# High weights against high and low input in three matmuls of 288, 512 and 288 columns, low sums apart in PSUM

## The chip, the cores and the metric

One NeuronCore of a Trainium2 chip runs the whole program. The metric is the device time of one execution in microseconds. Five engines take part: TensorE (PE: matmuls, PEld: its weight loads), VectorE (DVE), ScalarE (ACT), GpSimd (POOL) and SyncE (SP, which issues the DMAs).

## The reference

One inference step of a 2-layer streaming encoder over 544 tokens (512 of a prompt, 32 of a sample), width 1024:

```python
x = x + jnp.concatenate([o_a, o_b, o_c, o_d], axis=-1) @ w_out
x = x + jnp.square(jax.nn.relu(rmsnorm(x, norm_mlp) @ mlp_w1)) @ mlp_w2
x = x + (pl @ ple_w_proj) * jax.nn.sigmoid(rmsnorm(x, norm_ple) @ ple_w_gate)
```

`o_a` to `o_d` are four head groups (gated DeltaNet, sliding-window attention, latent attention, a short gated convolution). `mlp_w1` is 1024 x 4096, `mlp_w2` 4096 x 1024, `ple_w_gate` 1024 x 1024. The inputs are float32, and so is the result.

## The kernel before

Activations lie feature-major: `x[128, 8, 544]`, features on partitions in 8 k-tiles (`KT`), tokens along the free axis. For float32 accuracy at the matmul's fast type (fp32r), each operand is split into a high part (rounded to fp32r) and a low part (what is left). A product is high x high + high x low + low x high, with the weights `whi` (high) and `wlo` (low) and the activations in `ha` and `hb`, shape `[128, 8, 2, 544]`, where index 0 of the third axis is the high part and 1 the low.

Weights come in units of 128 output features x 1024 inputs (512 KB in float32). For each unit SyncE loads `raw`, ScalarE writes `whi` (`high`, L642), GpSimd writes `wlo` (`rest`, L559), and TensorE runs `product` (L1330): for each of 8 k-tiles six matmuls of 272 columns (half of the 544 tokens, `HALF`), that is `whi` with both halves of the high part, `whi` with both halves of the low part, `wlo` with both halves of the high part, 48 in all. Both halves of a product sum up in two PSUM banks; consecutive products alternate between two pairs of banks. `raw`, `whi` and `wlo` have two slots each: the unit after next can be split only when the present product is through (ScalarE waits for `proj`), and its `wlo` must be there before its product.

A layer has 23 units of the input projection with the attention and DeltaNet work between them, then 8 of the output projection, then the MLP in 4 groups (`GROUPS`): 8 up products (`ha` to hidden features), then 8 down products (`hb` to x), and then the gates: twice four short products of the per-layer input (`ple_out`, 12 matmuls each) and four gate products of 48. Then comes the next layer, or the final norm.

The order on every engine is written out by hand and in-order; semaphores tie the engines together. What the change touches:

- TensorE: `product` L1330 (used by MLP and gates too), `sum_x` L1315 (sum of squares over the partitions for the rms), `first_units` L1350 (the next layer's first two products).
- VectorE, up products (`mlp_group`): L1180 takes relu of the PSUM sum times rms and frees the bank, L1182 squares, `split_to` casts to the high part (L914) and subtracts for the low part (L915), which signals `hidden`. The first down product waits, k-tile by k-tile, for the `hidden` tile of the same number.
- VectorE, down products: `add_out` L1167 adds the sum to x. In the last group `norm_high` (ScalarE, L659) and `norm_split` (VectorE, L909) then split x for the gates, and `square_x` (L665) and `add_square` (GpSimd, L571) sum the squares.
- VectorE, gates: L1296 multiplies the PSUM sum by rms, a memset (L1297) signals `gate_in`, ScalarE takes the sigmoid (L874), VectorE multiplies by `ple_out` (L1280) and adds to x (L1281). L1288 copies `ple_out` out of PSUM.
- GpSimd, gates: its queue alternates `rest` of a coming weight with `add_square` of a finished x tile, in that order by hand.

## Time and profile before

| | |
|---|---|
| median of 3 runs | 1681.04 us (1680.88 to 1682.52) |
| the profiled execution, its own time | 1682.13 us |
| its span (first to last instruction) | 1680.3 us |
| matmul instructions | 14582 |
| TensorE busy, share of the span | 94% |
| VectorE, ScalarE, GpSimd busy | 55%, 29%, 38% |

The page is one profiled execution. Its 40 slices are 42 us each: layer 0 takes the first 20, layer 1 the others. Matmuls overlap in the records (a matmul of 272 columns is shown with about 0.29 us, while the next one starts long before its end), so pace is read from start to start: of a merged row "start, us, xcount" it is (us minus one matmul's duration) / (count - 1). A square bracket behind a row is the idle time of that engine before it, and what ended it.

### The profile page before, as it was taken

Reading aid. Unit: us, or ns where it says so; the run is one execution under the profiler, and the core shown is the slowest. Engines: PE = TensorE matmul, PEld = TensorE weight load, DVE = VectorE, ACT = ScalarE, POOL = GpSimd, SP = SyncE. Lnnn points to the kernel's source line nnn. Section 1 sums busy time; section 2 is a strip of 40 time slices with the busy share of each in tenths; the row PEclk is TensorE's granted clock in tenths of the full one; section 3 lists DMA queues with packets and bytes.
Section 4 is the critical chain, followed back from the end, with each engine's and each line's share of the span. In section 5 each row is a group of like instructions: output and inputs, shape, how many; then the busy total and the mean of one; then the engine's idle time right before and its main releaser. Section 6 shows DMA issues by size and latency. Waiting matters only on the chain. (4 is left out here: it accounts for less than half of the span.)

```text
span 1680.3 us, 33063 instructions
## 1 busy us (share of the span) xinstructions
PE 1579.9 (94%) x14582; PEld 1494.3 (89%) x14582; DVE 925.7 (55%) x1474; ACT 495.2 (29%) x836; POOL 639.6 (38%) x313
## 2 busy tenths in 40 slices
PE   6899998799999999999888999988999999999996
PEld 6789776599999999999887897867999999999995
DVE  6765477456536171654576646764473544527553
ACT  6521333432111111133444313334311111111332
POOL 3235111054444343455532531111644444444652
PEclk9899999899999999999999999998999999999998
DMA  5111010122222232232321111101222222222221
GB/s 194 58 39 40 27 51 26 44 80 85 88 89 89 88 89 89 88 89 76 93 76 51 39 40 35 43 27 56 89 87 88 86 89 85 89 86 88 89 87 66
DMA packets 43806, 122.63 MB, mean 73 GB/s; under 512 B 10960, under 2 KB 13776, under 8 KB 43536
## 3 DMA queue, kind: packets, MB, share of 16 engines
q1 hardware_dynamic: 43520, 118.74, 22.9%
q8 instruction: 115, 1.88, 0.5%
q10 hardware_dynamic: 144, 1.78, 0.3%
q14 instruction: 27, 0.22, 0.1%
HBM read 116.75 MB, written 3.76 MB: 72 GB/s over the span
## 5 line engine op out<-in xcount | busy, mean ns | idle before, releaser
L1330 PE MATMUL psum_p<-hidden,w_high 128*128 128x272 f32 x5952 | 1003.0, 290 | 17.9 <-POOL w_rest L559 7.9
L1330 PEld LDWEIGHTS psum_p<-hidden,w_high 128*128 128x128 f32 x5952 | 846.7, 189 | 23.7 <-POOL w_rest L559 14.5
L559 POOL TENSOR_TENSOR w_rest<-raw,w_high 128x1024 fp32r<-128x1024 f32 x210 | 512.6, 2441 | 910.2 <-ACT w_high L642 910.2
L1330 PE MATMUL psum_p<-hidden,w_rest 128*128 128x272 f32 x2976 | 616.9, 288 | 0.0
L1330 PEld LDWEIGHTS psum_p<-hidden,w_rest 128*128 128x128 f32 x2976 | 467.2, 189 | 0.0
L642 ACT ACTIVATE w_high<-raw 128x1024 fp32r<-128x1024 f32 x210 | 222.5, 1060 | 823.1 <-PE psum_p L1330 791.7
L1167 DVE TENSOR_TENSOR x<-psum_p,x 128x544 f32<-128x544 f32 x80 | 58.0, 725 | 281.1 <-PE psum_p L1330 281.1
L914 DVE CAST hidden<-rope 128x544 fp32r<-128x544 f32 x64 | 157.3, 2457 | 2.2
L909 DVE SCALAR_TENSOR_TENSOR hidden<-x,parameters,hidden 128x544 fp32r<-128x544 f32 x48 | 90.7, 1889 | 44.4 <-ACT hidden L659 44.2
L1180 DVE SCALAR_TENSOR_TENSOR rope_in<-psum_p,rms 128x544 f32<-128x544 f32 x64 | 46.4, 725 | 109.0 <-PE psum_p L1330 100.4
L571 POOL TENSOR_TENSOR x_squares_summed<-x_squares_summed,x_squared 128x544 f32<-128x544 f32 x43 | 72.6, 1689 | 53.2 <-ACT x_squared L665 47.1
L1365 PE MATMUL psum_p<-hidden,w_high 128*128 128x272 f32 x512 | 92.7, 304 | 0.0
L1365 PEld LDWEIGHTS psum_p<-hidden,w_high 128*128 128x128 f32 x512 | 73.3, 193 | 6.8 <-issue 6.2
L1500 PEld LDWEIGHTS psum_p<-constants,probs 128*64 128x64 f32 (+4 forms) x200 | 19.2, 127 | 49.8 <-DVE probs L1146 34.7
L1500 PE MATMUL psum_p<-constants,probs 128*64 128x128 f32 (+4 forms) x200 | 34.6, 274 | 26.3 <-ACT probs_t L741 13.6
L727 ACT ACTIVATE probs<-psum_t,softmax_columns 128x192 f32<-128x192 f32 (+7 forms) x76 | 34.5, 454 | 64.9 <-DVE softmax_columns L1133 64.9
L1365 PE MATMUL psum_p<-hidden,w_rest 128*128 128x272 f32 x256 | 53.5, 290 | 0.0
L589 POOL TENSOR_TENSOR factor_t<-lower_t,constants 128x384 f32<-128x384 f32 x30 | 35.7, 1217 | 35.3 <-PE psum_t L1380 35.3
L1182 DVE TENSOR_TENSOR rope<-rope_in 128x544 f32<-128x544 f32 x64 | 46.9, 733 | 2.2
L915 DVE TENSOR_TENSOR hidden<-rope,hidden 128x544 fp32r<-128x544 f32 x64 | 46.4, 725 | 2.2
L665 ACT ACTIVATE x_squared<-x 128x544 f32<-128x544 f32 x56 | 36.3, 648 | 36.2 <-DVE x L1281 35.1
L943 DVE SCALAR_TENSOR_TENSOR conv_out<-conv_in,parameters,conv_out 128x547 f32<-128x547 f32 x36 | 44.9, 1247 | 1.3
(251 smaller groups left out, 1434.4 us busy)
## 6 DMA issues: line engine op xcount, KB each, us to landing
raw<-w_units SPq DMA_DIRECT2D x210, 512.0 KB, 3.5
x<-x_t SPq DMA_DIRECT2D x8, 272.0 KB, 6.4
y_t<-y SPq DMA_DIRECT2D x8, 272.0 KB, 2.1
constants<-consts ACTq DMA_DIRECT2D x1, 1737.5 KB, 9.1
ple_in<-p_t SPq DMA_DIRECT2D x2, 544.0 KB, 5.2
w_kv<-w_kv SPq DMA_DIRECT2D x2, 256.0 KB, 5.3
ckv_p<-mla_c SPq DMA_DIRECT2D x2, 256.0 KB, 2.7
mla_c<-ckv_cache SPq DMA_DIRECT2D x2, 128.0 KB, 5.1
```

Source lines behind the costliest of these rows:

```text
L559: mark(pool.tensor_tensor(wlo[:, s, :], raw[:, ring(l, u, RAW), :], whi[:, s, :].bitcast(F32), ALU.subtract), lo_done)
L571: ins = pool.tensor_tensor(sumx[:], sumx[:], sqx[:, m % 2, :], ALU.add)
L642: mark(act.activation(whi[:, n % SPLIT, :], raw[:, n % RAW, :], ACT.Copy), hi_done)
L909: mark(dve.scalar_tensor_tensor(ha[l][:, m, 1, :], x[:, m, :], g, f(ha[l][:, m, 0, :]), ALU.mult, ALU.subtract), normed)
L914: step(dve.tensor_copy(dst(0), src), l)
L915: mark(dve.tensor_tensor(dst(1), src, f(dst(0)), ALU.subtract), sig)
L1167: link(dve, dve.tensor_tensor(two(x[:, m, :]), psum_of(l, o), two(x[:, m, :]), ALU.add), freed, l)
L1180: link(dve, dve.scalar_tensor_tensor(two(xr[:]), psum_of(l, o), 0.0, two(rms[:]), ALU.max, ALU.mult), freed, l)
L1182: step(dve.tensor_tensor(t1[:], xr[:], xr[:], ALU.mult), l)
L1330: ins = pe.matmul(pp[:, 2 * b + h, 0:HALF], w[:, s, cols(k)], rhs[:, k, part, h * HALF:(h + 1) * HALF], start=(n == 0 and z == 0), stop=(n ...
L1365: ins = pe.matmul(pp[:, h, 0:HALF], w[:, s, k * P:(k + 1) * P], ha[l][:, k, half, h * HALF:(h + 1) * HALF], start=(k == 0 and z == 0), sto ...
L1500: ins = pe.transpose(pp[0:n, 2, b * P:b * P + rows], prob[0:rows, t % 3, k0:k0 + n], ident[0:rows, 0:rows])
```

## The change

For the MLP's 64 products and the 8 gate products of each layer, `joined_product` takes the place of `product`. The activations are laid out anew: the 1088 values of a k-tile are four quarters of 272, high first half, low first half, low second half, high second half. `whi` meets them in three matmuls of 288, 512 and 288 columns, which are written as one run across three PSUM banks, and `wlo` meets the two outer quarters (high) in two matmuls of 272. So the outer quarters of the run in PSUM hold high x high + low x high, and the inner two hold high x low. Whoever reads a result adds them:

- up: ScalarE copies the inner quarters to `sqt` (`rest_copy`), VectorE adds the outer ones to it, takes relu and rms, squares; ScalarE writes the high part (`hidden_high`) where VectorE cast it, and VectorE subtracts. ScalarE's queue gets `rest_copy` ahead of `high` and `hidden_high` behind it.
- down: two additions to x instead of one.
- gates: a copy, an addition and a multiplication by rms instead of one multiplication and the memset.

Products of the output projection and of `ple_out` keep their six matmuls but use other banks, the sums of squares of phases 1 and 2 use banks 0 and 1, and TensorE waits for the last DeltaNet state ahead of the output projection.

```diff
+EDGE = (2 * TOK - 512) // 2
+        ps = ctx.enter_context(nc.psum_tensor("psum", [P, 8, 512], F32))
+        pp, pt = ps[:, 0:4, :], ps[:, 4:8, :]
...
+        def bank(l, o):
+            return (5, 2)[slot(l, o)] if o >= U_OUT else 2 * slot(l, o)
+        def joined(l, o):
+            at = 512 * bank(l, o) + 512 - EDGE
+            return ps[:].rearrange("p b c -> p (b c)")[:, at:at + 2 * TOK]
+        def quarters(ap):
+            return ap.rearrange("p (q t) -> p q t", t=HALF)
+        def high_of(h, m):
+            return quarters(h[:, m].rearrange("p a t -> p (a t)"))[:, 0:4:3, :]
+        def rest_of(h, m):
+            return quarters(h[:, m].rearrange("p a t -> p (a t)"))[:, 1:3, :]
...
+            def rest_copy(l, g, i):
+                o = U_MLP + g * 2 * KT + i
+                act.wait_ge(*proj.at(l, o + 1))
+                if i or g:
+                    act.wait_ge(*freed.at(l, o if i else o - KT))
+                mark(act.activation(two(sqt[:]), quarters(joined(l, o))[:, 1:3, :], ACT.Copy), rest_out)
+            def hidden_high(l, g, i):
+                act.wait_ge(*hid_raw.at(l, g * KT + i + 1))
+                mark(act.activation(high_of(hb[l], i), two(t1[:]), ACT.Copy), hid_high)
...
+                for g in range(GROUPS):
+                    for i in range(2 * KT):
+                        if i < KT:
+                            rest_copy(l, g, i)
+                        high(l, U_MLP + SPLIT + i + 2 * KT * g)
+                        if g == 0 and i == 0:
+                            inv_rms(l, 1)
+                        if i < KT:
+                            hidden_high(l, g, i)
+                        elif g == GROUPS - 1:
+                            norm_high(l, 2, i - KT)
+                            square_x(l, 2, i - KT)
...
+            def add_joined(l, o, m):
+                dve.wait_ge(*proj.at(l, o + 1))
+                acc = quarters(joined(l, o))
+                step(dve.tensor_tensor(two(x[:, m, :]), acc[:, 0:4:3, :], two(x[:, m, :]), ALU.add), l)
+                link(dve, dve.tensor_tensor(two(x[:, m, :]), acc[:, 1:3, :], two(x[:, m, :]), ALU.add), freed, l)
...
                     dve.wait_ge(*proj.at(l, o + 1))
-
-                    link(dve, dve.scalar_tensor_tensor(two(xr[:]), psum_of(l, o), 0.0, two(rms[:]), ALU.max, ALU.mult),
+                    dve.wait_ge(*rest_out.at(l, g * KT + i + 1))
+                    link(dve, dve.tensor_tensor(two(xr[:]), quarters(joined(l, o))[:, 0:4:3, :], two(sqt[:]), ALU.add),
                          freed, l)
-                    step(dve.tensor_tensor(t1[:], xr[:], xr[:], ALU.mult), l)
-                    split_to(l, lambda z: hb[l][:, i, z, :], t1[:], hidden)
+                    step(dve.scalar_tensor_tensor(xr[:], xr[:], 0.0, rms[:], ALU.max, ALU.mult), l)
+                    mark(dve.tensor_tensor(t1[:], xr[:], xr[:], ALU.mult), hid_raw)
+                    dve.wait_ge(*hid_raw.now(l))
+                    dve.wait_ge(*hid_high.at(l, g * KT + i + 1))
+                    mark(dve.tensor_tensor(rest_of(hb[l], i), two(t1[:]), f(high_of(hb[l], i)), ALU.subtract), hidden)
                 for m in range(KT):
-                    add_out(l, U_MLP + g * 2 * KT + KT + m, m)
+                    add_joined(l, U_MLP + g * 2 * KT + KT + m, m)
...
+                    gate = [xr, sqt][m % 2][:]
+                    acc = quarters(joined(l, o))
                     dve.wait_ge(*proj.at(l, o + 1))
-                    link(dve, dve.tensor_tensor(two([xr, sqt][m % 2][:]), psum_of(l, o), two(rms[:]), ALU.mult), freed, l)
-                    mark(dve.memset(t1[:, 0:1], 0.0), gate_in)
+                    step(dve.tensor_copy(two(gate), acc[:, 0:4:3, :]), l)
+                    link(dve, dve.tensor_tensor(two(gate), acc[:, 1:3, :], two(gate), ALU.add), freed, l)
+                    mark(dve.tensor_tensor(gate, gate, rms[:], ALU.mult), gate_in)
...
+            def joined_product(l, u, o, rhs, ready):
+                s, acc = ring(l, u, SPLIT), joined(l, o)
+                pe.wait_ge(*lo_done.at(l, u + 1))
+                pe.wait_ge(*freed.at(l, o - 1))
+                for k in range(KT):
+                    if ready is not None:
+                        ready(k)
+                    w, src = whi[:, s, k * P:(k + 1) * P], rhs[:, k].rearrange("p a t -> p (a t)")
+                    for t0, t1_ in ((0, EDGE), (EDGE, EDGE + 512), (EDGE + 512, 2 * TOK)):
+                        pe.matmul(acc[:, t0:t1_], w, src[:, t0:t1_], start=(k == 0),
+                                  stop=(k == KT - 1 and t0 == EDGE))
+                    w = wlo[:, s, k * P:(k + 1) * P]
+                    for t0 in (0, 2 * TOK - HALF):
+                        ins = pe.matmul(acc[:, t0:t0 + HALF], w, src[:, t0:t0 + HALF], start=False, stop=(k == KT - 1))
+                mark(ins, proj)
...
                 pe.wait_ge(*orn.at(l, 2))
+                pe.wait_ge(*s_dve.at(l, NCH))
```

## Rows read from the trace of the kernel before

**Rows 1.** The page: busy time, its 40 slices and the clock's, the last chain.
```profile
PE 1579.9 (94%) x14582; PEld 1494.3 (89%) x14582; DVE 925.7 (55%) x1474; ACT 495.2 (29%) x836; POOL 639.6 (38%) x313
...
PE   6899998799999999999888999988999999999996
...
PEclk9899999899999999999999999998999999999998
...
PE 40%; DVE 6%; ACT 2%; issue 1%; POOL 0%; POOLq 0%; DVEq 0%; ACTq 0%
```

**Rows 2.** The last chain in order of time, layer 1's MLP: start us, us, what.
```profile
1217.56 379.69 PE psum_p L1330 x3024
```

**Rows 3.** Timeline of PE (start, us, line, xcount) at four places; two lines' durations (ns).
```profile
10.87 1.11 PE L1350 MATMUL psum_p<-hidden,w_high 128*128 128x272 f32 x4
11.78 0.43 PE L1350 MATMUL psum_p<-hidden,w_rest 128*128 128x272 f32 x1
...
1216.48 1.08 PE L1315 MATMUL psum_t<-x_squares_summed,constants 128*128 128x272 f32 x4
...
L1315 PE MATMUL psum_t<-x_squares_summed,constants x24: 390/392/393, 24.3 to 1612.0; 128*128 128x272 f32 x24
...
L1565 PE MATMUL psum_p<-mla_c,w_kv x16: 499/499/603, 186.8 to 1016.0; 128*128 128x400 f32 x16
...
1095.54 0.27 PE L1500 MATMUL psum_p<-constants,probs 128*128 128x128 f32 x1
...
1135.23 0.60 PE L1500 MATMUL psum_p<-constants,probs 128*128 128x128 f32 x4
```

**Rows 4.** Timeline from 602 to 607 us: one up product's end and its hidden tile.
```profile
602.10 0.41 PE L1330 MATMUL psum_p<-hidden,w_rest 128*128 128x272 f32 x2
...
602.35 0.67 PE L1330 MATMUL psum_p<-hidden,w_high 128*128 128x272 f32 x4
602.55 0.73 DVE L1180 SCALAR_TENSOR_TENSOR rope_in<-psum_p,rms 128x544 f32<-128x544 f32 x1 [1.23 <-PE psum_p L1330]
602.61 1.07 ACT L642 ACTIVATE w_high<-raw 128x1024 fp32r<-128x1024 f32 x1 [4.96 <-PE psum_p L1330]
...
603.31 0.72 DVE L1182 TENSOR_TENSOR rope<-rope_in 128x544 f32<-128x544 f32 x1
...
603.75 2.54 POOL L559 TENSOR_TENSOR w_rest<-raw,w_high 128x1024 fp32r<-128x1024 f32 x1 [3.49 <-ACT w_high L642]
...
604.07 2.52 DVE L914 CAST hidden<-rope 128x544 fp32r<-128x544 f32 x1
...
606.62 0.72 DVE L915 TENSOR_TENSOR hidden<-rope,hidden 128x544 fp32r<-128x544 f32 x1
```

**Rows 5.** Groups over the whole span (busy us, mean ns), and one line's durations (ns).
```profile
L1167 DVE TENSOR_TENSOR x<-psum_p,x 128x544 f32<-128x544 f32 x80 | 58.0, 725 | 281.1 <-PE psum_p L1330 281.1
...
L665 ACT ACTIVATE x_squared<-x 128x544 f32<-128x544 f32 x56 | 36.3, 648 | 36.2 <-DVE x L1281 35.1 <-DVE x_squares_summed L1217 1.0
...
L809 ACT ACTIVATE mla_v<-psum_p x6: 597/598/598, 191.8 to 1020.8; 128x512 f32<-128x512 f32 x6
```

**Rows 6.** Timeline, end of layer 1's MLP: an operation of two SBUF operands meets GpSimd.
```profile
1598.47 2.40 POOL L559 TENSOR_TENSOR w_rest<-raw,w_high 128x1024 fp32r<-128x1024 f32 x1 [1.82 <-ACT w_high L642]
...
1599.13 2.32 DVE L909 SCALAR_TENSOR_TENSOR hidden<-x,parameters,hidden 128x544 fp32r<-128x544 f32 x1 [1.13 <-ACT hidden L659]
```

**Rows 7.** Timeline of the gates: layer 1's gate 4; last, the next layer's first product.
```profile
1643.10 0.72 DVE L1296 TENSOR_TENSOR rope_in<-psum_p,rms 128x544 f32<-128x544 f32 x1 [5.76 <-PE psum_p L1330]
...
1648.30 2.36 POOL L559 TENSOR_TENSOR w_rest<-raw,w_high 128x1024 fp32r<-128x1024 f32 x1
...
1650.72 0.77 PE L1330 MATMUL psum_p<-hidden,w_high 128*128 128x272 f32 x4 [1.70 <-POOL w_rest L559]
...
840.92 0.77 PE L1350 MATMUL psum_p<-hidden,w_high 128*128 128x272 f32 x4 [1.51 <-POOL w_rest L559]
```

**Rows 8.** Waits of PE over the span: us in total, times, longest us.
```profile
PE psum_p L1330 <- DVE ple_out L1288: 6.3, 4, 2.0
```

55 lines of the change are left out of this document (25 added, 30 removed).

## The prediction

> **What bounds the kernel now.** I read the page first: TensorE is busy 94% of the span, its granted clock is 9 tenths or more in nearly every slice, and the chain that ended last lies 40% on it [rows 1]. The chain in order of time then says where it is alone: in layer 1 one stretch of 379.69 us is nothing but 3024 matmuls of L1330 [rows 2], 63 products of 48. So in the MLP no other engine ends a wait, and what an edit saves on TensorE comes back one to one, unless a new wait appears. The pace there is 379.69 / 3024 = 0.1256 us per matmul, 6.03 us per product of 48, 0.7534 us per k-tile of six. The stream of 272 columns at 2.4 GHz is 113.3 ns, so 12.3 ns per matmul are something else.
>
> **What the 12.3 ns are.** At the low clock (1.2 GHz) the same matmul is spaced (11.78 - 10.87) / 4 = 227 ns, and 272 / 1.2 = 226.7: nothing on top [rows 3]. The plain fp32 passes of L1315 (272 columns, two cycles each, 226.7 ns) are spaced (1.08 - 0.39) / 3 = 230 ns, about 3 on top [rows 3]. A weight load that nothing hides costs 603 - 499 = 104 ns [rows 3], and L1500, with 128x128 weights and short streams, runs at (0.60 - 0.27) / 3 = 110 ns per matmul [rows 3]. So a load fits under 113 ns, and the 12.3 ns show only where a column is streamed each cycle at 2.4 GHz. No row has an fp32r matmul of another length, so three readings stay: a fixed price per matmul, a slower stream per column (0.462 ns instead of 0.417), or a floor of some 125 ns per load and matmul that a long stream hides. The first leans on weight loads and matmuls being the only things that come once per instruction; I take it.
>
> The skill bears on this. The Trainium skill (TensorE: Matmul & The Clock Gate, section Back-to-back issue gap) gives a warm spacing of N / 2.4 + 2.5 ns. The plain passes agree (230 against 229.2); the fp32r matmuls don't (125.6 against 115.8), and the measurement decides. With 2.5 ns per matmul the pace term below would be -2.9 us instead of -14.2.
>
> **The change, part by part.**
>
> 1. *TensorE's stream.* A k-tile of six matmuls of 272 columns becomes 288 + 512 + 288 + 272 + 272: 1632 columns as before, five matmuls. 64 MLP units and 8 gate units in each of two layers, 8 k-tiles each: 1152 k-tiles. At a fixed 12.3 ns each loses 12.3 ns: -14.2 us; a k-tile is 0.741 us, a product 5.93. Bounds: 0 (per column), and -40.6 us (floor: 288 columns stay at 125.6, 512 take 213.3 + 3 = 216.3; 4 x 125.6 + 216.3 = 718.7, 35 ns less per k-tile).
>
> 2. *The hidden chain.* Today, after an up product is done at 602.55 [rows 4]: VectorE evacuates (0.73), squares (0.72), casts (2.52) and subtracts (0.72), and is through at 607.34, 4.79 us after the start. The cast isn't work but a wait: it ends 0.30 us after GpSimd's subtraction (603.75 + 2.54 = 606.29). The next product's first matmul starts at 602.35, and when it is the first down product it wants the eighth hidden tile at its eighth k-tile, 7 x 0.753 = 5.27 later, at 607.62. So today the chain is covered by 0.28 us less a hand-over: almost nothing.
> After the change, from the same zero (602.55 = 0), on ScalarE, which starts at 0.06 [rows 4]: rest_copy of 544 from PSUM, 0.63 (512 take 0.598 [rows 5]), to 0.69. VectorE adds (0.725, one operand in PSUM like L1167 [rows 5]) 0.72 to 1.45, then relu and rms with both operands in SBUF 1.48 to 2.26. ScalarE splits the next weight 0.69 to 1.75; GpSimd comes at 1.82, while VectorE's operation of two SBUF operands runs, and does its 2.26 us (604.03 to 606.29 in [rows 4]) from 2.26 to 4.52. The squaring also has two SBUF operands and asks at 2.29: such an operation that finds GpSimd at work ends 0.58 after it (L909: 1599.13 + 2.32 = 1601.45 against 1598.47 + 2.40 = 1600.87 [rows 6]), so at 5.10. hidden_high on ScalarE takes 0.65 (L665, 544 elements [rows 5]) to 5.78, the subtraction 0.73 to 6.54. With 0.07 for the hand-over and 0.08 for a weight load that had to wait, TensorE goes on at 6.69. It could have at -0.20 + 7 x 0.741 = 4.99. The wait is 1.7 us, once for each change from up to down: 4 groups, 2 layers, 8 x 1.7 = +13.6 us. Bounds: 0, if the squaring gets in ahead of GpSimd, and 8 x 2.4 = 19, if rest_copy is late too. Between other up products nothing waits: ScalarE's own loop, 0.06 to 5.78, is inside 5.93, and GpSimd has the next weight's rest ready at 4.52. That is knife-edge: were a product faster than 5.75, ScalarE would set the pace.
>
> 3. *Down products.* Two additions of 0.725 instead of one [rows 5], in a product of 5.93, with no reader before the next group: 0. In the last group the split of x for the gates runs behind them; each split still ends 0.58 us after GpSimd's operation [rows 6], whatever VectorE added before it: 0.
>
> 4. *Gates.* VectorE has a copy, an addition and a multiplication (3 x 0.73) where it had 0.72 and a memset: +1.4 us ahead of the sigmoid. This chain isn't covered. For gate 4 of layer 1 it runs from 1643.10 over sigmoid, product, x, square and GpSimd's sum to GpSimd's rest of a later weight, 1648.30 to 1650.66, and TensorE stood 1.70 us for it; before layer 1's first product it stood 1.51 [rows 7]. TensorE also waits for ple_out, up to 2.0 us at a time, behind VectorE's queue [rows 8], in which gate 3's chain now stands longer. Per layer: +1.4 before gate 4 (ple_out), +1.4 before gate 6, +1.4 at the end (next layer's first unit; in layer 1 the final sum), and at gate 3, whose weight waits on ScalarE behind gate 0, somewhere between 0 and those 1.4, of which I take 0.3: 4.5, twice: +9. Bounds +4 (half hidden) and +18 (the new multiplication by rms, again two SBUF operands, meets GpSimd's 2.4 us at half of the gates). Nothing excludes the upper one.
>
> 5. *The rest.* Banks, statistics in other banks, the wait for the state update ahead of the output projection (done long before): 0 with no reason for either sign. ScalarE's first rms of an MLP is 0.63 later, but the PSUM release behind it comes at 0.63 + 1.06 + 2 x 0.65 + 0.73 = 3.8 us, and TensorE wants that bank at 5.93.
>
> Sum: -14.2 + 13.6 + 9 = +8.4. The profiled execution took 1682.13 us (span 1680.3), the median of the runs is 1681.04, 1.1 less; the sum is small against it, so I add it to the median: **1689.5 us**, span about 1689.
>
> **Rivals.**
> - *The stream pays per column.* Then part 1 is 0, part 2 stays (8 x 1.6 = 13), part 4 stays: +22, 1703 us. For it: the 12.3 ns vanish at the low clock, as they would if the operand came at no more than one column in 0.462 ns. Against it: nothing in the rows shows such a rate by itself.
> - *Not slower: the floor.* A long stream hides the 12 ns and more; part 1 is -40.6, but up products are held at about 5.80 by ScalarE's loop (gives 3 back), the wait at the change to down grows to 1.9 (15), gates as above: -40.6 + 3 + 15 + 9 = -14, 1667 us. It decides from 20 ns saved per k-tile on. The skill's formula (same page and section), for 288 and 512 columns alone and the measured 125.6 for the two of 272, would make a k-tile 712 ns: this rival. For it: plain passes have hardly anything on top. Against: the load takes 104, not 125.
> - *The lock misses.* VectorE squares before GpSimd takes hold; the chain is through at 3.02 + 0.03 + 0.65 + 0.03 + 0.73 = 4.5, before 4.99, and nothing waits at the change to down: -14.2 + 9 = -5, 1676 us. Against: VectorE's cast in [rows 4] asked 0.04 us after the operation before it and still came second.
> - *The clock falls.* Gate waits grow past 3 us, and behind each some 25 matmuls (an estimate) are at 227 instead of 126 ns [rows 2, 3]: 2.5 us each, four places, on top of the forecast: +18, 1699 us. Against it: the page's clock digits are 9 through layer 0's gates now [rows 1].
>
> **How the numbers follow.** Forecast 0.42, per column 0.18, floor 0.22, lock misses 0.10, clock 0.08. A measurement of this kernel can tell about 0.2% from no change, 3.4 us: faster is below 1677.7, slower above 1684.4. The floor and the missed lock are mostly faster (0.29 with their tails), the forecast's lower edge and halves of these within (0.14), the rest slower (0.57). The range goes from the floor rival to just past the per-column one: 1667 to 1704; the forecast's own is 1681 to 1698.
>
> **What would show it.** In the long stretch: spacing of the k-tile 741 ns (754: per column; 719: floor). At the eight changes from up to down: TensorE idle 1.7 us before the eighth k-tile, released by VectorE's subtraction, and a squaring of 2.8 us that ends 0.58 after GpSimd. In the gates: waits for w_rest and ple_out longer by 1.4 each. What would make me wrong: a squaring of 0.73 us, or matmuls of 512 columns spaced 216 with short ones below 125.

## The result, and the profile after

The changed kernel takes 1702.3 us (median of 4 runs, 1700.9 to 1705.18) against 1681.78 us for the kernel before, measured beside it: ratio 1.0118, 95% interval 1.0102 to 1.0134. It is slower by 20.5 us; 8.4 were forecast. Its profiled execution took 1705.18 us (span 1703.4), 3 us above its own median.

The page: first line busy time of the span, then the clock's 40 slices.

```profile
PE 1581.1 (93%) x13430; PEld 1440.9 (85%) x13430; DVE 1009.3 (59%) x1554; ACT 572.9 (34%) x964; POOL 660.7 (39%) x313
...
PEclk9899999899999999999998999997999999999997
```

TensorE has 1152 matmuls fewer than in [rows 1], one for each k-tile, and its busy time is no smaller. VectorE works 84 us more and ScalarE 78. Where that matters is in TensorE's waits (us in total, times, longest us):

```profile
PE psum L1405 <- DVE hidden L1239: 11.6, 8, 1.4
...
PE psum L1405 <- POOL w_rest L588: 8.4, 5, 3.1
```

L1405 holds the three joined matmuls of each k-tile. The first line did not exist before: eight waits for the hidden tile, one for each change from up to down products. The second is at the gates.

The starts of TensorE's phases in the two timelines say how the span's 23.1 us are spread (us, differences of starts within one trace):

| stretch | before | after | difference |
|---|---|---|---|
| MLP, both layers | 386.62 + 386.62 | 390.09 + 390.08 | +6.9 |
| PLE and gates, layer 0 to layer 1's first matmul | 69.82 | 75.04 | +5.2 |
| PLE and gates, layer 1 to the last matmul | 72.81 | 80.60 | +7.8 |
| layer 1, from its first product to its MLP | 369.54 | 372.50 | +3.0 |
| the rest | | | +0.2 |

**The hidden chain**, timeline from 602.9 us, the stretch of [rows 4] (start us, us, engine, line):

```profile
604.23 0.63 ACT L697 ACTIVATE squares<-psum 128x544 f32<-128x544 f32 x1 [0.22 <-PE psum L1409]
...
604.75 1.05 ACT L671 ACTIVATE w_high<-raw 128x1024 fp32r<-128x1024 f32 x1
...
604.96 0.72 DVE L1233 TENSOR_TENSOR rope_in<-psum,squares 128x544 f32<-128x544 f32 x1
...
605.52 0.66 PE L1405 MATMUL psum<-hidden,w_high 128*128 128x288 f32 x3
605.72 0.72 DVE L1235 SCALAR_TENSOR_TENSOR rope_in<-rope_in,rms 128x544 f32<-128x544 f32 x1
605.88 2.83 POOL L588 TENSOR_TENSOR w_rest<-raw,w_high 128x1024 fp32r<-128x1024 f32 x1 [3.14 <-ACT w_high L671]
...
606.48 2.82 DVE L1236 TENSOR_TENSOR rope<-rope_in 128x544 f32<-128x544 f32 x1
...
609.33 0.66 ACT L702 ACTIVATE hidden<-rope 128x544 fp32r<-128x544 f32 x1 [3.52 <-DVE rope L1236]
...
610.09 0.73 DVE L1239 TENSOR_TENSOR hidden<-rope,hidden 128x544 fp32r<-128x544 f32 x1 [0.80 <-ACT hidden L702]
...
611.50 0.66 PE L1405 MATMUL psum<-hidden,w_high 128*128 128x288 f32 x3
...
623.44 0.66 PE L1405 MATMUL psum<-hidden,w_high 128*128 128x288 f32 x3
```

The squaring (L1236) asks at 606.48, finds GpSimd at work and ends at 609.30, 0.59 us after GpSimd's 608.71. The chain runs from 604.23 to 610.82, 6.59 us. The first and the last PE row are 24 k-tiles apart: 17.92 us, 746.7 ns a k-tile, where [rows 2] give 753.4.

What that chain costs at a change from up to down, timeline of TensorE: the first down product of layer 0's second group begins at 530.63, its eighth k-tile waits, and the next product begins at 538.32.

```profile
530.63 0.66 PE L1405 MATMUL psum<-hidden,w_high 128*128 128x288 f32 x3
...
537.46 0.77 PE L1405 MATMUL psum<-hidden,w_high 128*128 128x288 f32 x3 [1.45 <-DVE hidden L1239]
...
538.32 0.66 PE L1405 MATMUL psum<-hidden,w_high 128*128 128x288 f32 x3
```

This product takes 7.69 us where its neighbours take 5.97, and so do the other seven like it: 1.71 us more, each time. In the kernel before, the first down product is no longer than the others (6.03).

**The gates**, the same place as [rows 7], behind gate 4 of layer 1:

```profile
1660.98 1.06 ACT L671 ACTIVATE w_high<-raw 128x1024 fp32r<-128x1024 f32 x1 [5.57 <-PE psum L1409]
1660.98 0.72 DVE L1354 COPY rope_in<-psum 128x544 f32<-128x544 f32 x1 [5.63 <-PE psum L1409]
1661.74 0.72 DVE L1355 TENSOR_TENSOR rope_in<-psum,rope_in 128x544 f32<-128x544 f32 x1
1662.50 0.72 DVE L1356 TENSOR_TENSOR rope_in<-rope_in,rms 128x544 f32<-128x544 f32 x1
1663.26 0.66 ACT L918 ACTIVATE rope_in<-rope_in 128x544 f32<-128x544 f32 x1 [1.23 <-DVE rope_in L1356]
...
1665.47 0.66 ACT L708 ACTIVATE x_squared<-x 128x544 f32<-128x544 f32 x1 [1.55 <-DVE x L1337]
1666.21 1.34 POOL L600 TENSOR_TENSOR x_squares_summed<-x_squares_summed,x_squared 128x544 f32<-128x544 f32 x1 [7.94 <-ACT x_squared L708]
...
1667.51 2.35 POOL L588 TENSOR_TENSOR w_rest<-raw,w_high 128x1024 fp32r<-128x1024 f32 x1
```

and TensorE there, with the granted clock of that stretch (windows: us, busy by engine, PEclk, DMA share, GB/s):

```profile
1669.91 1.27 PE L1405 MATMUL psum<-hidden,w_high 128*128 128x288 f32 x3 [3.06 <-POOL w_rest L588]
...
1669.00:1675.00 6.00, 5.09 (x18) 4.71 (x19) 2.88 (x3) 1.31 (x2) 2.45 (x3) 0.50 0.00 0
```

Gate 4's sum to GpSimd's w_rest took 5.20 us in [rows 7] (1643.10 to 1648.30) and takes 6.53 now. GpSimd's queue has the sum of squares ahead of that subtraction, though w_high was there at 1662.04. TensorE waits 3.06 us where it waited 1.70, and then runs at 0.50 of its clock, the 1.2 GHz level, until about 1675.7: 21 matmuls.

### The profile page after: what moved, and what is told of

Read it like the earlier page. It is cut to its first block and busy times, and to the rows that moved or that the text cites. A ratio compares the mean times of both kernels' runs of the same rounds, so it can differ in the third digit from the quotient of the medians.

```text
span 1703.4 us, 31149 instructions
## 1 busy us (share of the span) xinstructions
PE 1581.1 (93%) x13430; PEld 1440.9 (85%) x13430; DVE 1009.3 (59%) x1554; ACT 572.9 (34%) x964; POOL 660.7 (39%) x313
## 5 line engine op out<-in xcount | busy, mean ns | idle before, releaser
L1405 PE MATMUL psum<-hidden,w_high 128*128 128x288 f32 (+1 forms) x3456 | 761.8, 328 | 21.6 <-DVE hidden L1239 11.6
L1405 PEld LDWEIGHTS psum<-hidden,w_high 128*128 128x128 f32 x3456 | 513.6, 189 | 25.1 <-DVE hidden L1239 13.3
L1409 PE MATMUL psum<-hidden,w_rest 128*128 128x272 f32 x2304 | 476.8, 288 | 0.0
L1409 PEld LDWEIGHTS psum<-hidden,w_rest 128*128 128x128 f32 x2304 | 370.1, 188 | 50.8
L1390 PE MATMUL psum<-hidden,w_high 128*128 128x272 f32 x1344 | 235.7, 298 | 12.0 <-DVE misc L970 4.7
L1390 PEld LDWEIGHTS psum<-hidden,w_high 128*128 128x128 f32 x1344 | 197.3, 195 | 17.0 <-POOL w_rest L588 10.3
L1236 DVE TENSOR_TENSOR rope<-rope_in 128x544 f32<-128x544 f32 x64 | 176.0, 2750 | 2.2
L1218 DVE TENSOR_TENSOR x<-psum,x 128x544 f32<-128x544 f32 x64 | 46.4, 725 | 214.9 <-PE psum L1409 214.9
L1390 PE MATMUL psum<-hidden,w_rest 128*128 128x272 f32 x672 | 142.2, 293 | 0.0
L702 ACT ACTIVATE hidden<-rope 128x544 fp32r<-128x544 f32 x64 | 42.2, 659 | 224.0 <-DVE rope L1236 224.0
L1390 PEld LDWEIGHTS psum<-hidden,w_rest 128*128 128x128 f32 x672 | 108.4, 194 | 0.0
L1442 PE MATMUL psum<-hidden,w_high 128*128 128x272 f32 x512 | 91.7, 301 | 0.0
L1442 PEld LDWEIGHTS psum<-hidden,w_high 128*128 128x128 f32 x512 | 72.5, 191 | 6.6 <-issue 6.0
L1233 DVE TENSOR_TENSOR rope_in<-psum,squares 128x544 f32<-128x544 f32 x64 | 46.4, 725 | 47.8 <-ACT squares L697 32.5
L697 ACT ACTIVATE squares<-psum 128x544 f32<-128x544 f32 x64 | 40.1, 626 | 49.5 <-PE psum L1409 49.5
```

Of the source, the lines that this page charges most:

```text
L1218: step(dve.tensor_tensor(two(x[:, m, :]), acc[:, 0:4:3, :], two(x[:, m, :]), ALU.add), l)
L1233: link(dve, dve.tensor_tensor(two(xr[:]), quarters(joined(l, o))[:, 0:4:3, :], two(sqt[:]), ALU.add), freed, l)
L1236: mark(dve.tensor_tensor(t1[:], xr[:], xr[:], ALU.mult), hid_raw)
L1390: ins = pe.matmul(ps[:, b + h, 0:HALF], w[:, s, cols(k)], rhs[:, k, part, h * HALF:(h + 1) * HALF], start=(n == 0 and z == 0), stop=(n == ...
L1405: pe.matmul(acc[:, t0:t1_], w, src[:, t0:t1_], start=(k == 0), stop=(k == KT - 1 and t0 == EDGE))
L1409: ins = pe.matmul(acc[:, t0:t0 + HALF], w, src[:, t0:t0 + HALF], start=False, stop=(k == KT - 1))
```

## The experiments

All times beside the kernel before on the same chip. "MLP" is the length of layer 0's MLP phase, "gates" of the PLE and gate phases of layer 0 and layer 1, read as in the table above.

| kernel | ratio, 95% interval | MLP | gates |
|---|---|---|---|
| before | 1 | 386.62 | 69.82, 72.81 |
| after | 1.0118 (1.0102 to 1.0134) | 390.09 | 75.04, 80.60 |
| gates_old | 1.0042 (1.0027 to 1.0056) | 390.09 | 69.83, 72.80 |
| gates_inner | 1.0038 (1.0022 to 1.0053) | 390.10 | 69.73, 74.10 |
| down_only | 0.9984 (0.9970 to 0.9998) | 384.99 | 71.35, 72.80 |
| act_square | 1.0060 (1.0039 to 1.0082) | 384.05 | 76.57, 79.34 |
| pool_waits | 1.0130 (1.0106 to 1.0154) | 388.96 | 78.13, 79.55 |
| act_sq_gates_old | 0.9978 (0.9967 to 0.9990) | 384.08 | 69.85, 72.81 |
| the same once more | 0.9972 (0.9961 to 0.9983) | 384.07 | 69.86, 72.82 |
| extra_copy | 1.0043 (1.0026 to 1.0059) | 386.65 | 71.17, 76.19 |
| sum_later | 1.0120 (1.0099 to 1.0141) | 390.10 | 75.71, 76.34 |
| before_sum_later | 1.0017 (1.0004 to 1.0030) | 386.63 | 72.28, 72.37 |
| best | 0.9977 (0.9965 to 0.9988) | 384.05 | 72.20, 72.37 |
| middle_first | 1.0126 (1.0107 to 1.0145) | 388.42 | 76.54, 79.21 |
| middle_best | 0.9990 (0.9978 to 1.0003) | 385.32 | 71.34, 72.80 |

### One part at a time: the gates undone, the down products alone

gates_old, the gate products and what reads them put back:

```diff
-                    step(dve.tensor_copy(two(gate), acc[:, 0:4:3, :]), l)
-                    link(dve, dve.tensor_tensor(two(gate), acc[:, 1:3, :], two(gate), ALU.add), freed, l)
-                    mark(dve.tensor_tensor(gate, gate, rms[:], ALU.mult), gate_in)
+                    link(dve, dve.tensor_tensor(two(gate), psum_of(l, o), two(rms[:]), ALU.mult), freed, l)
+                    mark(dve.memset(t1[:, 0:1], 0.0), gate_in)
...
-                    joined_product(l, U_PLE + 1 + m + m // 4, U_PLE + 4 * (m // 4 + 1) + m, ha[l],
+                    product(l, U_PLE + 1 + m + m // 4, U_PLE + 4 * (m // 4 + 1) + m, ha[l], range(KT),
```

> The changed kernel with its eight gate products per layer put back as before: six matmuls of 272 columns per k-tile, one multiplication per product straight out of PSUM, and the old layout of the normalised input of that phase. The up and down products stay joined. Nothing is left out. By the phases of the two traces the gate products (the time from the first matmul of the PLE phase to the next layer's first, and to the last matmul) cost 5.2 us in layer 0 and 6.4 + 1.4 us in layer 1, 13.0 us of the 20.5. Theory (the chain on VectorE behind each gate product is what costs): 1702.3 - 13 = 1689 us, with the steps of 8.3 us between gate products back at 6.3 to 7 and TensorE's granted clock at 1.00 from gate 6 of layer 1 on. Rival (a late transfer or GpSimd's preparation of the weights sets the gates' pace, the sums only meet it): over 1698.

1.0042: the gates cost 0.76% of 1682, 12.8 us, with the gate phases back at 69.83 and 72.80, the lengths of before. That the late weight sets their pace whatever the sums do is out.

down_only, the kernel before with only this (and the hidden tile laid out for it):

```diff
-                        product(l, u, u, hb[l], range(KT),
-                                ready=(lambda k: pe.wait_ge(*hidden.at(l, g * KT + k + 1))) if m == 0 else None)
+                        joined_product(l, u, u, hb[l],
+                                       (lambda k: pe.wait_ge(*hidden.at(l, g * KT + k + 1))) if m == 0 else None)
```

> The kernel before with one part of the change alone: the 64 down products per program run (8 in each of 4 groups and 2 layers) in three matmuls of 288, 512 and 288 columns and two of 272 per k-tile, read with one addition more. Up and gate products as before, so no product whose sum is waited for is touched but the last of each layer. 512 k-tiles change. The changed kernel's trace shows a k-tile at 0.747 us against 0.753 of before: 512 x -0.0065 = -3.3 us, 1678.4. By the forecast's 12.3 ns per matmul saved it would be 512 x -12.3 = -6.3 us, 1675.4; by a purely per-column cost of 0.462 ns it would be +10, 1692. If the extra addition on the evacuation of a down product were on the path, the PE's gaps ahead of the next product would show it.

0.9984, -2.7 us (-5.0 to -0.3); the MLP phases are shorter by 1.6 and 1.7 us, 6.4 ns for each of 2 x 256 k-tiles (from product to product, 753.4 ns a k-tile become 746.7). The term that was forecast at 12.3 ns is about half as large, and a gain all the same; the second addition costs nothing that shows. (The 1.5 us more at layer 0's gates are a granted clock of 0.65 from 809 to 813 us in this execution; the gates' code is that of before.)

### Is it the chain or the joined form?

gates_inner leaves the joined gate matmuls and shortens what reads them:

```diff
-                    step(dve.tensor_copy(two(gate), acc[:, 0:4:3, :]), l)
-                    link(dve, dve.tensor_tensor(two(gate), acc[:, 1:3, :], two(gate), ALU.add), freed, l)
-                    mark(dve.tensor_tensor(gate, gate, rms[:], ALU.mult), gate_in)
+                    link(dve, dve.tensor_tensor(two(gate), acc[:, 1:3, :], two(rms[:]), ALU.mult), freed, l)
+                    mark(dve.memset(t1[:, 0:1], 0.0), gate_in)
```

> The changed kernel with joined gate products, whose result VectorE reads by one operation only: the inner two quarters times rms, straight out of PSUM (0.72 us), as before the change; the low sums in the outer quarters are left out of the gates. It parts the two halves of the gates' cost: matmuls and layout are those of the change, the chain behind them is that of before. Theory (only the chain on VectorE costs): as with the gate products undone, less the stream's gain of 128 k-tiles x 6.5 ns = 0.8: 1702.3 - 14 = 1688.5, ratio 1.0035. Rival (the joined form itself costs, by its banks, its longer accumulation or the strided layout of the input): over 1695, ratio 1.008 or more.

The text has the quarters the wrong way round: the inner ones hold the low sums, so what is left out of the gates is the outer, main sums. The operations and their sizes are as told. 1.0038 with joined matmuls against 1.0042 with the old ones: the joined form costs nothing that shows, the chain behind it costs 13 us. (Layer 1's gate phase is 1.3 us longer than before here, and the granted clock was 0.50 from 1659 to 1662 in this execution, behind a wait of 1.75 us at gate 6.)

extra_copy lengthens the same chain in the kernel before:

```diff
+                    step(dve.tensor_copy([...], psum_of(l, o)), l)
                     link(dve, dve.tensor_tensor([...], psum_of(l, o), two(rms[:]), ALU.mult), freed, l)
```

> The kernel before with one VectorE copy more per gate product, out of PSUM into the tile that the multiplication then overwrites: 0.72 us and a handover, 0.76 more in each of the 16 gate chains, all else as before. Nothing is left out. It measures the price of a longer gate chain by itself. The change puts two such operations in (1.5 us) and costs 13 to 14 us there. Theory (the price runs through the chain, part at the two late waits in each layer, part at the last product, and falls short of the low clock): +3 to +6 us, ratio 1.002 to 1.0035. Rival (joined matmuls or their layout cost the gates, not the chain): under +1.

+7.2 us (4.4 to 9.9) for 16 copies of 0.76, above the top of what was expected; the gate phases grew by 1.35 and 3.4, and layer 1's first units by 1.5. In layer 1 a part of it is the clock:

```profile
1655.13 1.27 PE L1331 MATMUL psum_p<-hidden,w_high 128*128 128x272 f32 x4 [2.38 <-POOL w_rest L559]
...
1656.65 1.11 PE L1331 MATMUL psum_p<-hidden,w_high 128*128 128x272 f32 x4
```

The second row's matmuls start 227 ns apart (1657.56 - 1656.65, by 4), the low level, behind a wait of 2.38 us where before waited 1.70 and stayed at 1.00.

### The squaring: does GpSimd hold it?

act_square moves it to ScalarE:

```diff
 def hidden_high(l, g, i):
     act.wait_ge(*hid_raw.at(l, g * KT + i + 1))
+    mark(act.activation(t1[:], xr[:], ACT.Square), hid_sq)
+    act.wait_ge(*hid_sq.now(l))
     mark(act.activation(high_of(hb[l], i), two(t1[:]), ACT.Copy), hid_high)
...
-                    mark(dve.tensor_tensor(t1[:], xr[:], xr[:], ALU.mult), hid_raw)
```

> The changed kernel with the squaring of the hidden values moved from VectorE to ScalarE, ahead of ScalarE's rounding of them. Nothing is left out. Theory (the squaring, the one operation of the hidden chain with both operands in SBUF, waits for GpSimd's running operation: 2.82 us against 0.72): the squaring takes 0.66 on ScalarE, the chain from the last up product's end to hidden ready falls from about 5.9 to some 3.8 + one handover of 0.1 us, so TensorE's waits of 1.4 to 1.7 us ahead of the down products at eight places go to under 0.2: -11 us, 1691. Rival (the addition that reads ScalarE's copy and the longer handovers cost it, not GpSimd): the waits stay over 1 us, time over 1698.

pool_waits keeps it on VectorE and makes GpSimd come after it:

```diff
                 for i in range(2 * KT * (GROUPS - 1)):
+                    if i % (2 * KT) < KT:
+                        pool.wait_ge(*hid_raw.at(l, i // (2 * KT) * KT + i % (2 * KT) + 1))
                     rest(l, U_MLP + SPLIT + i)
```

> The changed kernel, whose only edit is one wait more on GpSimd: in the up products it starts the subtraction that makes a unit's w_rest only when VectorE's squaring of that product's hidden values is done (hid_raw). Engines, operations and data are as in the changed kernel. Theory (VectorE's operation with both operands in SBUF waits for GpSimd's running one): without GpSimd beside it the squaring takes 0.72 instead of 2.82 us, hidden is ready about 2 us earlier and the PE's waits ahead of the down products fall from 1.4 to 1.7 us to none or to what the later w_rest costs: it is then ready some 5.4 us after the product's end, inside the 5.98 of a product. 1702.3 - 10 = 1692, like the kernel with the squaring on ScalarE. Rival (what ScalarE saved there was something else than GpSimd's hold, say VectorE's own load): squaring stays over 2 us, time 1700 or more. If w_rest comes too late for the next product, the waits go to TensorE <- w_rest and the time rises instead.

Timeline of act_square, one product, and of pool_waits, one product:

```profile
594.54 0.73 DVE L1238 SCALAR_TENSOR_TENSOR rope_in<-rope_in,rms 128x544 f32<-128x544 f32 x1
594.70 2.83 POOL L589 TENSOR_TENSOR w_rest<-raw,w_high 128x1024 fp32r<-128x1024 f32 x1 [3.14 <-ACT w_high L672]
...
595.30 0.66 ACT L703 ACTIVATE rope<-rope_in 128x544 f32<-128x544 f32 x1 [0.68 <-DVE rope_in L1238]
...
595.99 0.66 ACT L705 ACTIVATE hidden<-rope 128x544 fp32r<-128x544 f32 x1
...
596.75 1.36 DVE L1241 TENSOR_TENSOR hidden<-rope,hidden 128x544 fp32r<-128x544 f32 x1 [1.49 <-ACT hidden L705]
```

```profile
602.75 0.72 DVE L1240 TENSOR_TENSOR rope<-rope_in 128x544 f32<-128x544 f32 x1
603.51 0.66 ACT L706 ACTIVATE hidden<-rope 128x544 fp32r<-128x544 f32 x1 [1.43 <-DVE rope L1240]
603.55 2.41 POOL L588 TENSOR_TENSOR w_rest<-raw,w_high 128x1024 fp32r<-128x1024 f32 x1 [3.56 <-DVE rope L1240]
604.27 2.27 DVE L1243 TENSOR_TENSOR hidden<-rope,hidden 128x544 fp32r<-128x544 f32 x1 [0.79 <-ACT hidden L706]
```

With the squaring on ScalarE, which GpSimd doesn't hold, the waits for the hidden tile are gone from the list of waits and the MLP is 6.0 us shorter per layer, 1.5 for each change (the first down product is 0.20 longer than its neighbours, not 1.71): 9.8 us in the time (1.0118 to 1.0060), 11 were expected. The final subtraction now meets GpSimd's end (1.36 us, to 598.11, 0.58 after 597.53), early enough to be covered.

In pool_waits the squaring takes 0.72, as the theory has it: nothing but GpSimd's time of coming was changed. The other half of the expectation fell. GpSimd's subtraction now lies over the next operation with two SBUF operands, which took 0.73 and takes 2.27, and hidden is ready hardly earlier: TensorE waits 7.2 us at the eight changes instead of 11.6, the MLP gains 1.1 us instead of 6, and the time is not below the changed kernel's. The hold had not been removed but moved. The Trainium skill (SBUF — State Buffer, section SBUF: two separate sides) calls the pair of ports that VectorE and GpSimd share an exclusive lock, held for a whole instruction, and names VectorE's operations with two SBUF inputs among those that need it; the two traces agree, and 0.58 us after GpSimd's end is what each held operation shows.

### Both together

act_sq_gates_old is gates_old and act_square at once:

> Both edits at once: gate products as before, squaring of the hidden values on ScalarE; up and down products joined as in the change. Nothing is left out. If the two costs add: 1702.3 - 13 - 11 = 1678, which would be below the kernel before (1681.8) by the stream's gain of the joined products (1024 k-tiles x 6.5 ns = 6.7 us) less what remains of waits. If the waits at the eight changes only move to another releaser: 1685 or more.

> The same as the earlier kernel with gate products as before and the squaring on ScalarE, once more, on the chip of the two others: ratio 0.9978 again (0.9967 to 0.999), so that the order of the matmuls is compared on one chip.

0.9978, and 0.9972 on another chip: 1679.8 against 1682.86 us, and 1679.65 against 1684.2. The two costs add (0.76 + 0.58 = 1.34%; both edits give 1.40 to 1.46%), and what is left, 0.2 to 0.3% faster than the kernel before, is the joined stream of 1024 k-tiles: its two MLP phases are 5.1 us shorter, about what the pace gives (6.9) less 0.2 at each of the eight changes.

### GpSimd's queue in the gates

sum_later exchanges two operations in that queue:

```diff
                     rest(l, u)
-                    if m:
-                        add_square(l, 3, m - 1)
+                    if m > 1:
+                        add_square(l, 3, m - 2)
+                add_square(l, 3, KT - 2)
```

> The changed kernel with one exchange in GpSimd's queue: in the PLE and gate phase it adds the squares of x of gate m only after the w_rest of the next unit but one, not ahead of it. Same operations. In the changed kernel's trace w_rest for gate 6 of layer 1 starts at 1667.51, right behind that addition, though w_high was ready at 1662.04; TensorE waits 3.06 us for it and then runs at half the clock. Theory (each gate's chain on VectorE reaches TensorE through this place in GpSimd's queue): the waits for w_rest at gates 6 and 7 of both layers go (8 to 9 us with the low clock), time 1693 to 1696. Rival (the later release of PSUM, or VectorE's own queue, makes the gates late): less than 3 us, 1699 or more. The weight's subtraction then runs beside VectorE's multiplication by rms or others with two SBUF operands, which may lengthen them by up to 2 us; that would give some of it back.

1.0120: no gain. The waits it aimed at went: gates 5, 6 and 7 start 5.98 us apart, no wait for w_rest among them. But (timeline, behind gate 4 of layer 1; then TensorE's first PLE product of the second four):

```profile
1664.81 2.40 POOL L588 TENSOR_TENSOR w_rest<-raw,w_high 128x1024 fp32r<-128x1024 f32 x1 [2.91 <-ACT w_high L672]
1665.20 2.59 DVE L1357 TENSOR_TENSOR rope_in<-rope_in,rms 128x544 f32<-128x544 f32 x1
...
1651.18 0.74 PE L1391 MATMUL psum<-ple_split,w_high 128*128 128x272 f32 x4 [2.23 <-DVE squares L1356]
```

the earlier subtraction catches the multiplication by rms (2.59 us for 0.72), PSUM is released later (2.23 us of waiting, 1.17 in the changed kernel), and gate 4 and the next layer start later: TensorE waits 5.34 us before layer 1's first product (1.99 in the changed kernel's trace), and with the granted clock at 0.50 behind it the first two products take 2.8 us more. The rival that was put down as giving some of it back gave most or all of it back: gate phases and first two products together are 0.8 us shorter than in the changed kernel's trace, and 2.4 to 2.8 shorter than in those of act_square, middle_first and order_mix, whose gates are the changed kernel's; the ratio, with 3.5 us to either side, can't tell that from nothing. So the chain reaches TensorE through this place in the queue, as the theory said, and closing it opens the next one. The same exchange in the kernel before, and in the fastest version:

> The kernel before with the one exchange in GpSimd's queue (sums of squares one place later in the gate phase), nothing of the change. It prices that exchange where the gate chain is short. Theory: TensorE's idle 1.70 us before gate 6 goes in both layers, -2 to -3.4 us, ratio 0.998 to 0.999. Rival: what the subtraction beside VectorE's multiplication and addition costs is as much: ratio 1.000 or above.

> Three edits on the changed kernel: gate products as before the change, squaring of the hidden values on ScalarE, and the sums of squares one place later in GpSimd's queue in the gate phase. Nothing is left out. The first two alone measured 0.9978 of the kernel before. In that kernel's trace TensorE still waits 9.4 us for w_rest at five places in the PLE and gate phases and the first units; the third edit starts w_rest for gates 6 and 7 some 4 us earlier (1.7 us each of TensorE's idle time before gate 6, two layers). Theory: 0.9978 less 2 to 3.4 us, 1676 to 1678 (0.996 to 0.997). Rival: as in the changed kernel with this edit, the subtraction now runs beside VectorE's additions and holds them (2.1 and 1.8 us where 0.72), which gives it all back at the layer change and the PLE products: 0.998 or more.

1.0017 (worse) and 0.9977 (no different from 0.9978). The old order, which looks like a mistake, keeps GpSimd off VectorE's chain; in the kernel before, the two gate phases of the traces say so too (142.6 us with the old order, 144.7 with the new).

### What a matmul costs by its length

lengths replaces seven of eight k-tiles in layer 1's MLP (the second layer):

```diff
+                    if length and k:
+                        for j in range(5):
+                            ins = pe.matmul(ps[:, bank(l, o) + j % 2, 0:length], w, src[:, 0:length], start=True, stop=True)
+                        continue
```

> A probe of TensorE's issue spacing by length: the changed kernel, in whose second layer the MLP products replace, of each eight k-tiles, seven by five matmuls each of one length (512 columns in group 0, 400 in group 1, 256 in group 2, 128 in group 3) on the same weights and inputs, going by turns to two PSUM banks; only one k-tile is summed as it should be, so the MLP of layer 2 is not computed and the time says nothing. Spacing of back-to-back starts by the three laws: fixed part plus columns (6.2 ns + 0.4385 ns a column, fitted to 272 and 512 of the changed kernel): 230.7, 181.6, 118.5, 62.3. The forecast's 12.3 ns fixed (then 0.416 a column): 225, 179, 119, 66. Purely per column (0.462): 236, 185, 118, 59. If a floor stands under the short ones (weight loads, issue), 128 shows it.

Timeline of TensorE in the four groups (starts, merged rows), two groups of instructions, and two windows of the last group (the granted clock stands third from the end):

```profile
1260.08 4.28 PE L1406 MATMUL psum<-hidden,w_high 128*128 128x512 f32 x18
...
1459.79 4.48 PE L1406 MATMUL psum<-hidden,w_high 128*128 128x400 f32 x24
...
1559.74 4.00 PE L1406 MATMUL psum<-hidden,w_high 128*128 128x256 f32 x32
...
1578.66 4.12 PE L1406 MATMUL psum<-hidden,w_high 128*128 128x128 f32 x35
...
1629.70 2.98 PE L1406 MATMUL psum<-hidden,w_high 128*128 128x128 f32 x13
...
L1406 PE MATMUL psum<-hidden,w_high 128*128 128x512 f32 x560 | 130.4, 391 | 0.0
...
L1406 PE MATMUL psum<-hidden,w_high 128*128 128x256 f32 x560 | 72.1, 288 | 7.2 <-DVE hidden L1239 4.0 <-POOL w_rest L588 3.2
...
1569.00:1585.00 16.00, 15.20 (x130) 14.72 (x128) 10.55 (x9) 4.80 (x7) 8.12 (x3) 1.00 0.29 99
1600.00:1660.00 60.00, 59.67 (x273) 58.90 (x272) 29.43 (x25) 15.91 (x21) 22.88 (x10) 0.50 0.19 62
```

A row ends with the last matmul's own time, so the spacing is (4.00 - 0.288) / 31 = 119.7 ns at 256 columns, and in the same way 180.1 at 400 (341 ns of its own) and about 228 at 512 ((4.28 - 0.391) / 17 = 228.8; the mean over the pairs of starts is 227.8, stops left out). At 2.4 GHz the columns alone are 106.7, 166.7 and 213.3: 13.0, 13.4 and 14.5 ns on top. So in a stream of one length the part per matmul is nearly fixed, as the forecast had it, and 0.462 ns a column (236) is out, and so is a floor that long streams hide (216). The fit to the changed kernel (118.5, 181.6, 230.7) misses too. The 128 columns need the clock beside them. At a granted 1.00 the starts are about 112 ns apart (the row at 1578.66, less one matmul's own 0.275: 3.845 / 34 = 113 ns), twice their columns (53.3): short matmuls with a weight load each take hardly less than those of 256. This is the price that L1500 shows in [rows 3], 110. From 1587 on the granted clock was 0.50, and there the same matmuls are 213 ns apart.

But then a k-tile should take 680 + 4 x 12.3 to 13 + 14.5 = 744 to 746.5 ns, and takes 746.7. The sum nearly comes out, but not its parts: in the changed kernel's MLP a 512 ahead of a 288 takes 230.9 ns (17.6 above its columns), a 288 ahead of a 272 takes 134.1 (14.1), and the three others 11.7 above their columns. order_mix asks for the order within the k-tile:

```diff
-                    for t0, t1_ in ((0, EDGE), (EDGE, EDGE + 512), (EDGE + 512, 2 * TOK)):
+                    cuts = ((0, EDGE), (EDGE, EDGE + 512), (EDGE + 512, 2 * TOK))
+                    for t0, t1_ in [cuts[j] for j in ((0, 1, 2), (1, 0, 2), (0, 2, 1), (2, 1, 0))[form]]:
```

> The changed kernel with the three matmuls of w_high in the MLP products in another order by group: group 0 as in the change (288, 512, 288 by place in PSUM: outer, middle, outer), group 1 middle first, group 2 the two outer ones and then the middle, group 3 the outer pair exchanged. Same matmuls, same sums. It asks why a k-tile takes 747 ns where 1632 columns at 2.4 GHz and the 13 ns a matmul of the probe of lengths would give 680 + 65 = 745, and the 12.3 of the forecast 741.5. If a change of length or bank costs (a 512 ahead of a 288 was 230.9 ns against 227.8 among its own), the orders differ by up to 4 ns a k-tile: 0.5 us a group of 128 k-tiles. If a matmul's own part alone counts, all four groups take the same within 0.2 us.

From product to product, stops left out, a k-tile takes 746.7 ns as in the change, 743.4 with the 512 first, 746.6 with it last, 743.4 with the outer pair exchanged, the same in both layers. So the order matters by 3.3 ns (the two forecasts that follow took 4.2). The lengths alone don't decide it: with the outer pair exchanged they follow each other as in the change, and what differs is which end of the input and of the sums in PSUM each 288 works on. Which of the two matters, no run tells. The gain was then taken at its word:

> The changed kernel with one exchange: in each k-tile of the joined products the 512-column matmul goes first, then the two of 288. Same matmuls and sums. In the mixed orders this k-tile took 743.4 ns against 747.6. Theory (the spacing is read one to one): 1152 x -4.2 ns = -4.8 us, 1697.5, ratio 1.009. Rival (a faster stream meets the same chain behind the up and gate products, as at the eight changes): the stretches that end in a wait gain nothing at their last product, and the ratio stays within 0.001 of 1.0118.

> The changed kernel with gate products as before, squaring of the hidden values on ScalarE, and the 512-column matmul first in each k-tile of the up and down products. Nothing is left out. Theory: 0.9978 (the same without the exchange) less 1024 k-tiles x 4.2 ns = 4.3 us, 0.0026: ratio 0.9952, some 1674 us. Rival (waits for the hidden values take it back, since w_rest and the hidden chain are timed by GpSimd and VectorE): ratio 0.997 to 0.998.

In middle_first all groups do run at 743.4 ns and each MLP is 1.7 us shorter (512 x 3.3 ns), but the ratio is 1.0126, not 1.009, and by the number it is the rival that came. -3.3 us cannot be told beside what the rest of the program did in those runs: the interval is 3.2 us to either side. In middle_best, which should have been the fastest, the ratio is 0.9990 and its profile shows why (timeline of TensorE; eight k-tiles between each two rows of a pair):

```profile
493.10 0.67 PE L1405 MATMUL psum<-hidden,w_high 128*128 128x512 f32 x3
...
499.18 0.67 PE L1405 MATMUL psum<-hidden,w_high 128*128 128x512 f32 x3
...
560.30 0.66 PE L1405 MATMUL psum<-hidden,w_high 128*128 128x512 f32 x3
...
566.25 0.66 PE L1405 MATMUL psum<-hidden,w_high 128*128 128x512 f32 x3
```

```profile
488.00:524.00 36.00, 36.00 (x238) 33.76 (x237) 16.83 (x18) 17.34 (x24) 16.95 (x6) 1.00 0.24 77
556.00:592.00 36.00, 36.00 (x244) 33.84 (x243) 9.71 (x14) 8.71 (x10) 14.69 (x7) 1.00 0.27 88
```

The same code at the same granted clock of 1.00 goes at 6.08 us a product in one stretch and 5.95 in the next, 760 against 743 ns a k-tile. It stays at one pace for whole products and passes from 760 to 743 near 536 us, at the eighth k-tile of a group's first down product, where the stream stops for a moment (a start 330 ns after the last) for the hidden tile. In this execution every passage from one pace to the other within an MLP, seven in the two layers, is at such a stop; at the eighth it kept its pace. 55 of the 128 products went at 760, and the two MLP phases took 385.32 and 386.39 us where the version without the exchange took 384.08 and 384.01, and 2.1 less was expected of each (1.7 by order_mix). What decides which pace follows a stop was not found.

## Why the prediction was right or wrong

**Direction and mechanisms** were right: slower, by a new wait at eight places and a longer chain at the gates. The size was off by 12.8 us (1702.3 for 1689.5; 0.7 of it is the kernel before, 1681.78 for 1681.04).

1. *TensorE's stream* is the term that was most mis-sized: -14.2 forecast; 1152 x 6.7 ns = -7.7 measured (746.7 against 753.4). The step that failed is "at a fixed 12.3 ns each loses 12.3 ns". The price per matmul is nearly fixed in a stream of one length, but it is not 12.3 for each of five in this mix: 17.6 for the 512 ahead of a 288, 14.1 for the 288 ahead of a 272, 11.7 for each of the other three, 66.8 in all where 61.5 was taken, and the order in the k-tile moves it. Nearly half of what the missing matmul saves goes there. Why these two cost more stays open. (The rival bound of -40.6 should read -40.0: 34.7 ns x 1152.)

2. *The hidden chain*: +13.6 forecast, +13.7 measured: each first down product is 1.71 us longer, eight times. Less the pace's gain of 1024 x 6.7 ns = 6.9, that makes 6.8, and the MLP phases grew by 6.9. Part by part it came as worked out: rest_copy 0.63, GpSimd ahead of the squaring, its end 0.58 to 0.59 after GpSimd's, the chain 6.59 after ScalarE's start (6.48 forecast). act_square shows the cause by taking it away, pool_waits by moving it.

3. *Down products*: 0 forecast, nothing seen (down_only).

4. *Gates*: +9 forecast (bounds 4 and 18), +13.0 in the profiled execution, 12.8 by gates_old. The places were right, and the prices are mostly the 1.4 of the forecast: the waits for w_rest before gate 6 grew by 1.36 in both layers, gate 4 came 1.7 and 2.4 later, the last matmul 1.3. The step that failed is that gate 3 was charged 0.3 and gate 7 nothing: gate 3 came 1.0 and 0.4 later, gate 7 0.8 and 2.5. (Layer 1's first product, charged at 1.4, came only 0.4 later.)

The 2.5 is the rival of the falling clock: after 3.06 us of waiting at gate 6 of layer 1 the granted clock was 0.50, for 21 matmuls (the forecast's 25 were an estimate that no row of the kernel before shows). After the same 3.06 us at gate 6 of layer 0 it stayed at 1.00, so such a wait allows the fall and doesn't force it. But the fall is the usual case: six traces have these gates (after, act_square, pool_waits, middle_first, order_mix, lengths), with twelve waits of 3.05 to 3.08 us before gate 6, and the granted clock fell to 0.50 behind ten of them. In the five others it also fell at layer 1's first product, behind a wait of 3.15 to 3.26 us (1.99 in the changed kernel's trace), and the first two products took 1.5 us more. A rival that got a chance of 0.08 is part of what the gates cost.

5. *The rest*: 0 forecast. Layer 1 from its first product to its MLP was 3.0 us longer in the profiled execution. TensorE's granted clock is 0.50 around the end of the state update in both kernels, but in the kernel before it was back at 1.00 when the output products began (1162), and in the changed kernel's profiled execution it stayed at 0.50 to 1177, 6 us into them. The same stretch took 369.5 to 375.4 us over these kernels, with the change's code 369.6 in gates_inner and 372.5 in gates_old, without it 369.5 in the kernel before and 373.4 in before_sum_later, so it belongs to an execution rather than to the change; it is about what this execution lies above the median.

Sum of what was measured: -6.9 (the MLP's 1024 k-tiles; the gates' 128 are in the 13.0) + 13.7 + 13.0 = +19.8, and the ratio of 1.0118 is +19.8 us (17.2 to 22.5).

The **per-column rival** named 1703, which is the time that came, for a wrong reason: the probe excludes its rate. Its number fits because nearly half of the forecast's gain was missing and the gates cost more. The **floor** is excluded by 228 ns at 512 columns. The **missed lock** is refuted by 62 of the 64 squarings of the changed kernel: each ends 0.58 us after GpSimd's subtraction and takes about 2.8 us. The other two, one in each layer (395.5 and 1233.1 us), had no GpSimd operation beside them and took 0.72.

## What to carry to other kernels

Before a sum is split so that it must be added on the way out, count the operations that come between the last matmul and whoever waits for the result, and charge them in full wherever that chain is not covered: 1.5 us more in 16 such places cost 13 us here, against 8 us for 1152 matmuls saved. An operation of VectorE that reads two SBUF operands should not stand where GpSimd is at work; giving it to ScalarE removed the wait, while shifting GpSimd, by a wait or in its queue, only moved the hold to the next such operation. A saving per matmul that is read off a stream of one length should be tried on the mixed stream before it is multiplied by a thousand.

## What the runs showed of the hardware that was not expected

- The spacing of fp32r matmuls of one length is columns at 2.4 GHz plus 13.0 (256), 13.4 (400) and 14.5 ns (512), and about 112 ns at 128 columns (lengths). In a mixed k-tile it depends on what stands beside it: a 512 took 230.9 ahead of a 288 and 234.1 ahead of a 272, 288 ones 128 to 134 (order_mix), and two k-tiles with the same sequence of lengths took 746.7 and 743.4.
- A mixed stream can hold two paces, 743 and 760 ns a k-tile, with the same code and the same granted clock, and changed over only where it was interrupted. Neither shows in the order of the changed kernel, whose groups all ran at 746.7.
- The granted clock fell to 0.50 behind waits of 1.75 us (gates_inner), 2.38 us (extra_copy) and 3.06 us, and stayed at 1.00 behind another of 3.06 us in the same execution as the last. It fell behind ten of twelve waits of that last kind.
